# Two of four raw-weight value units split into halves, and the sample group's attention one step earlier

## The reference, cut to what matters

```
q, k, v, qi, ki, wi = split(rmsnorm(x) @ w_attn_in)     # 1024 -> 3 x 1024 + 256 + 64 + 4
score = sum over 4 index heads of relu(qi . ki) * wi * scale, causal
idx   = top-k keys of score (64)                        # prompt and sample
# prompt: softmax attention over the picked keys of its 256 positions
# sample: cached keys and values of the 64 picked rows are gathered through
#         page_table, the new key is added if it was picked; softmax attention
h += o @ w_attn_out
```

## Time and profile before

| | |
|---|---|
| median of 3 runs | 594.36 us |
| the profiled execution | 595.13 us, of which the span is 593.3 us and 1.8 us lie around it |
| PE busy | 579.7 us (98% of the span) |
| DVE, ACT, POOL busy | 457.0, 369.8, 227.0 us (77%, 62%, 38%) |
| granted clock of TensorE, mean | 0.998 |

### The profile page before, as it was taken

How to read it: one execution, slowest core, us unless ns; L and a number is a source line. 1 busy time by engine, 2 the same in 40 slices (tenths; PEclk the granted TensorE clock), 3 DMA queues, 4 the chain that set the end, 5 groups by cost and what they waited for, 6 DMA issues and landing times.

```text
span 593.3 us, 12746 instructions
## 1 busy us (share of the span) xinstructions
PE 579.7 (98%) x5015; PEld 502.0 (85%) x5015; DVE 457.0 (77%) x904; ACT 369.8 (62%) x629; POOL 227.0 (38%) x230
## 2 busy tenths in 40 slices
PE   7999998999999999999999999999999999999995
PEld 6888887988888888888888888888888888888885
DVE  5899899466897887788678897889888778785542
ACT  6984566576675656565555788856765656564322
POOL 4241458723354545451011112264554545432220
PEclk9999999999999999999999999999999999999999
DMA  9949668319876767688997962065766767779602
GB/s 269 268 124 285 198 186 259 102 50 297 237 205 191 201 187 202 190 234 233 265 275 204 248 179 73 1 178 153 207 203 190 203 188 206 227 213 244 180 7 74
DMA packets 205420, 113.28 MB, mean 191 GB/s; under 512 B 5561, under 2 KB 202217, under 8 KB 205337
## 3 DMA queue, kind: packets, MB, share of 16 engines
q1 hardware_dynamic: 203169, 106.33, 63.8%
q0 software_dynamic: 1680, 5.79, 2.9%
q10 hardware_dynamic: 512, 0.35, 0.2%
HBM read 108.83 MB, written 3.86 MB: 190 GB/s over the span
## 4 chain that ended last, share of the span: by engine, by line
PE 87%; DVE 6%; DMA 2%; POOL 2%; ACT 1%; issue 1%; DVEq 0%; SPq 0%; ACTq 0%
PE acc L1536 24%; PE acc L1539 24%; PE acc L1542 24%; PE acc L1507 2%; DVE w_lo L998 2%; DMA area<-in_cache_v,gix 1%; PE acc L1727 1%; PE acc L1729 1%; PE acc L1728 1%; PE misc L1898 1%; DVE area L1137 1%; DMA area<-in_x_prompt 1%; POOL hT L1931 1%; ACT w_hi L594 1%; PE misc L1664 1%
## 5 line engine op out<-in xcount | busy, mean ns | idle before, releaser
L1536 PE MATMUL acc<-aH,w_hi 128*128 128x264 f16 (+1 forms) x886 | 244.5, 276 | 0.8 <-DVE work L1311 0.7
L1539 PE MATMUL acc<-aL,w_hi 128*128 128x264 f16 (+1 forms) x886 | 244.5, 276 | 0.0
L1542 PE MATMUL acc<-aH,w_lo 128*128 128x264 f16 (+1 forms) x886 | 244.5, 276 | 0.0
L998 DVE SCALAR_TENSOR_TENSOR w_lo<-stage,w_hi 128x1024 f16<-128x1024 f32 (+1 forms) x155 | 206.6, 1338 | 30.5 <-ACT w_hi L594 30.2
L594 ACT ACTIVATE w_hi<-stage 128x1024 f16<-128x1024 f32 (+1 forms) x155 | 171.1, 1110 | 31.7 <-PE acc L1542 25.2
L1536 PE MATMUL acc<-zH,w_hi 128*128 128x264 f16 x384 | 106.0, 276 | 0.0
L1539 PE MATMUL acc<-zL,w_hi 128*128 128x264 f16 x384 | 106.0, 276 | 0.0
L1542 PE MATMUL acc<-zH,w_lo 128*128 128x264 f16 x384 | 106.0, 276 | 0.0
L1539 PEld LDWEIGHTS acc<-aL,w_hi 128*128 128x128 f16 (+1 forms) x886 | 88.1, 99 | 13.5
L1536 PEld LDWEIGHTS acc<-aH,w_hi 128*128 128x128 f16 (+1 forms) x886 | 86.8, 98 | 14.5 <-issue 1.4
L1542 PEld LDWEIGHTS acc<-aH,w_lo 128*128 128x128 f16 (+1 forms) x886 | 88.1, 99 | 12.6
(11 more groups left out here) (421 smaller groups left out, 952.4 us busy)
## 6 DMA issues: line engine op xcount, KB each, us to landing
stage<-in_w_ffn_up SPq DMA_DIRECT2D x88, 512.0 KB, 4.7
stage<-in_w_ffn_down SPq DMA_DIRECT2D x32, 704.0 KB, 5.9
stage<-in_w_attn_in SPq DMA_DIRECT2D x22, 512.0 KB, 5.8
stage<-in_w_rec_in SPq DMA_DIRECT2D x16, 512.0 KB, 4.9
stage<-in_w_attn_out SPq DMA_DIRECT2D x8, 512.0 KB, 4.2
stage<-in_w_rec_out SPq DMA_DIRECT2D x8, 512.0 KB, 3.8
area<-in_w_attn_in SPq DMA_DIRECT2D x4, 512.0 KB, 4.8
area<-in_x_prompt SPq DMA_DIRECT2D x2, 512.0 KB, 4.9
```

What stands on the lines that cost most here:

```text
L998: v.scalar_tensor_tensor(low, stage[:, place_in_line(u) % 4, 0:n, 0:cols], WSCALE, high, ALU.mult, ALU.subtract).then_inc(lo_done, 1)
L1536: t_.matmul(out, high[:, c, :], xH[:, x0 + c, :], start=first and c == 0, stop=False)
L1539: t_.matmul(out, high[:, c, :], xL[:, x0 + c, :], start=False, stop=False)
L1542: ins = t_.matmul(out, low[:, c, :], xH[:, x0 + c, :], start=False, stop=last and c == n - 1)
```

## The change

`RAW_V` keeps the units 15 and 16 (v4 and v5); the units 13 and 14 (v2 and v3) are loaded into `stage`, split and multiplied like all others. By `SPLIT_AT` their `hi` and `lo` come at steps 9 and 10, ahead of the rounds of `take_merged` in these steps. On POOL all four gathers of values follow those of the keys at step 16, after unit 16 is done, and `biases` move from step 17 to step 19, with a wait for both gathers. `sample_dots` are at step 15 (one, before the `lo`), 16 (one before and one after it) and 17. The transposition of their result is after unit 20, the maximum at DVE's step 20, Exp at ACT's step 21, `turn_weights` inside unit 22, `pb` at step 22, and `sample_values` inside the units 23 and 24. `turn_picked` stays inside unit 14.

```
-RAW_V = U_V[2:6]
+RAW_V = U_V[4:6]
 SPLIT_AT = {u: u - SLOTS for u in range(SLOTS, U_OUT + SLOTS) if u not in RAW_V}
...
-VALUES_AT = 18
...                                                     (ACT)
-                if u == 22:
+                if u == 21:
                     act.wait_ge(smx_done, 1)
                     nc.scalar.activation(sl[:], sl[:], ACT.Exp).then_inc(sexp_done, 1)
...                                                     (DVE)
-                if u == 23:
+                if u == 22:
                     dve.wait_ge(sp_turned, 1)
...
-                if u == 16:
-                    sample_dots(0)
+                if 15 <= u < 17:
+                    sample_dots(u - 15)
                 if u != INSIDE:
                     for x in splits_of_step(u):
                         lo(x)
...
-                if 16 <= u < 19:
-                    sample_dots(u - 15)
-                if u == 21:
+                if 16 <= u < 18:
+                    sample_dots(u - 14)
+                if u == 20:
                     dve.wait_ge(sl_turned, 1)
...                                                     (PE)
-                    if u in (24, 25):
-                        between = lambda i: sample_values(4 * (u - 24) + i // 4, i % 4)
+                    if u in (23, 24):
+                        between = lambda i: sample_values(4 * (u - 23) + i // 4, i % 4)
...
-                    elif u == 23:
+                    elif u == 22:
                         between = lambda i: turn_weights() if i == 8 else None
...
-                if u == 21:
+                if u == 20:
                     pe.wait_ge(qb_read, 4)
                     pe.wait_ge(r0_kept, 1)
...                                                     (POOL)
                 if u == RAW_V[-1]:
                     pool.wait_ge(searched, 2)
                     for j in range(4):
                         gather(a["cache_k"], kgat, kg_in, j)
                     pool.wait_ge(unit_done, RAW_V[-1] + 1)
-                if u == RAW_V[-1] + 1:
+                    for j in range(4):
+                        gather(a["cache_v"], vgat, vg_in, j)
+                if u == RAW_V[-1] + 3:
                     for j in range(4):
                         pool.wait_ge(kg_in[j], 16)
+                        pool.wait_ge(vg_in[j], 16)
                     pool.wait_ge(roped, before(u) + 1)
                     biases()
-                if VALUES_AT <= u < VALUES_AT + 4:
-                    gather(a["cache_v"], vgat, vg_in, u - VALUES_AT)
```

## The result

The changed kernel takes **597.42 us** in the median of six runs (596.19 to 597.63), the kernel before 594.51 us in six runs (594.34 to 595.11). The ratio is 1.0042 with a 95% interval of 1.0029 to 1.0055: 2.5 us slower by the ratio and 2.9 by the medians, where 0.25 us were forecast. The profiled execution took 597.48 us, its span is 595.7 us.

A forecast was written before the change was run, and what follows sets the result against it. PE was taken as the bound, busy 579.7 of 593.3 us. +2.8 (end of unit 14) - 2.75 (four holes) + 0.2 (`pb`) = +0.25, so 594.36 + 0.25 = 594.6 us, range 593.6 to 596.6.

The forecast's parts named there:

- The search late by 3.48 us: On DVE, hi and lo of units 13 and 14 ahead of the search delay round 7 by 3.48 us.
- The hole at the turn, 4.7 us: Inside unit 14, PE stands at turn_picked from 61.1 to 65.8, waiting for POOL's row numbers: 4.7 us.
- Unit 14 ends 2.8 us later: On PE, unit 14 ends at 67.5 against 64.70, 2.8 us later, with the 1.72 saved included.
- first rival: Units 14 and 15 may run at half clock behind the 4.7 us hole: 1.6 us lost, 596.2 us, chance 0.28.
- The four holes given back, 2.75 us: PE's four waits in the edited stage, 1.2, 0.4, 0.3 and 0.2 us listed, were worth 2.75 us together.
- the hole at k2: PE's wait behind unit 21 for the rope of step 19, 1.34 us without a start, would be gone.
- the 0.2 us at `turn_weights`: PE's smallest hole: the maximum is done by about 93.5, PE asks at 94.0; the 0.2 goes or stays.
- DVE "hardly later" at the rope of step 19: DVE's rope of step 19, at 87.51 before, would come at 87 to 88, hardly later than now.
- The 2 us of slack: POOL's rope of step 19 ends by 89.6 and PE asks at 91.6, with 2 us to spare.
- `pb`, +0.2: pb, moved to DVE's step 22, ends at 97.2 against a need at 97.05: a new hole of 0.2.
- Nothing is given back: Rival: DVE or POOL stay late through step 21 and the holes move: +2.8, 597.2 us, chance 0.08.
- the search isn't late: Rival: PE has no new hole, 1.72 and up to 2.75 us are saved: 589.9 us, chance 0.04.

The follow-up runs named there:

- the moves alone: The changed kernel with all four value units raw again, keeping only the moved gathers, dots and softmax: 591.94 us, ratio 0.9951 to the kernel before.
- The splits alone: The kernel before with only the raw units cut from four to two, gathers, dots and softmax left in place: 600.12 us, ratio 1.0086.

## Why the prediction was wrong

- **The search late by 3.48 us:** right, to the digit (1.11 + 0.09 of waiting, twice 1.14).
- **The hole at the turn, 4.7 us:** right (4.62 idle, 66.38 - 0.45 = 65.93 against 65.8).
- **Unit 14 ends 2.8 us later:** this is the step that failed. It let the 11 matmuls behind the hole, and unit 15, run at full clock. They ran at 1.2 GHz until about 71.0, and filling the hole with matmuls, which doesn't let the turn start earlier, took 2.1 us off the kernel. The prediction had that mechanism as its first rival, with 596.2 us and a chance of 0.28, and held against it that there was one example only. The mean clock says that it was the case in all six runs, each at 0.995 or below. Its price, 1.6 us from the warm-up rows, was 0.5 too low. It took 0.127 us as the full-clock distance of two warm-up records; in the filling, at a granted clock of 1.00, 32 records start (3.73 - 0.27) / 31 = 0.112 apart, and with that the same sum is 27 x 0.073 = 2.0. (The granted clock reads 1.00 over those first warm-up records too, so this price rests on their distance alone.) With 1.6 even the rival and the top of the range (596.6) lie under the result.
- **The four holes given back, 2.75 us:** right in the sum, as the moves alone show: 594.88 - 591.94 = 2.9 us beside the same runs of before. The reason given for the largest was half wrong: I let "PE later by 2.8" help to close the hole at k2. The splits alone leave that hole at 1.2 us; the moves close it. And the 0.2 us at `turn_weights` didn't go: with the moves alone PE waits there for POOL's `biases` (0.2, line 1712).
- **DVE "hardly later" at the rope of step 19:** wrong. It was 2.5 us later than before (90.0), and still 1.6 later with the hole filled and the full clock (88.97 + 0.15 = 89.1). The 2 us of slack that the forecast had for k2 covered it; for k1, whose rope now has one block of dots more ahead of it, no slack had been worked out, and there the new wait of 0.5 us came.
- **`pb`, +0.2:** no wait of PE at the products with `pb` in any profile with the moves. In its place came POOL's `biases` in front of `turn_weights` (0.6) and the rope of k1 (0.5), seen once PE isn't slowed by the clock. Without the clock the change costs 0.5 us by the ratio (0.0 to 1.0), where 0.25 was forecast; that the two are so near is in part luck, as the sum didn't have these two waits.
- **"Nothing is given back" and "the search isn't late":** both refuted, by the waits after.

So the large terms were found and sized, and the forecast chose the wrong side of one question: whether an idle stretch of PE inside dense work costs only its length.

## What to carry to other kernels

Price a new wait of TensorE by its length and by the half clock that follows it: in these runs it came on top in a part of the executions at 1.9 us of idleness and in every profile with 2.7 us or more, for 1 to 2 us. Before work is added to an engine that "isn't the bound", look at its list ahead of the latest thing that the bounding engine asks of it; DVE was 77% busy and had no hole for 17 us. And test the halves of a mixed edit apart: here one was worth -0.5% and hid behind the other's +0.9%.

## What the runs showed of the hardware

The granted clock can fall after TensorE is back at work: with a hole of 2.8 us that ended at 66.2 it fell at about 67.4, with the 2.9 us hole that ended at 86.8 in the run with the turn in unit 15 at about 87.3, and with the 4.6 us hole that ended at 65.75 in the run with the splits alone at 66.2. In the changed kernel, with a hole of the same 4.6 us, it fell inside the hole. And float32 warm-up matmuls of ones by ones, 32 records in 3.7 us, held it at 2.4 GHz over a wait of 4.7 us.
